# Hybrid layer with a hierarchical mixture of experts: one SiLU table in the expert loop, routing maxima in one pass, and the last projected rows in halves

## The reference, cut to what matters

```
h   = x + mix @ w_out                       # 1024 x 1024
t   = rms_norm(h, g)                        # h * rsqrt(mean(h*h) + eps) * g
g_logits = t @ w_rg + b_rg                  # 4 groups;    grp = argmax, p_grp = softmax(g_logits)[grp]
e_logits = t @ w_re + b_re                  # 16 experts, viewed as 4 groups of 4
e_in     = e_logits[grp]                    # the 4 experts of the chosen group
top_p, top_i = top_k(softmax(e_in), 2);  top_p = top_p / sum(top_p)
y  = sum over e of combine[:, e] * ( silu(t @ w_gate[e]) * (t @ w_up[e]) ) @ w_down[e]
out = h + y
```

## Time and profile before

| | us |
|---|---|
| median of 3 runs | 902.34 (901.07 to 904.18) |
| the profiled execution | 902.31 |
| its span | 900.5 |
| busy: TensorE, VectorE, ScalarE, GpSimd | 846.6, 623.4, 572.2, 234.7 |
| mean granted TensorE clock | 0.987 |

### The profile page before, as it was taken

One profiled execution on the slowest core, in us unless ns is written; L12 is line 12 of the kernel. 1 busy time (PEld: TensorE's weight loads), 2 busy tenths in 40 slices (PEclk: granted clock), 3 DMA queues, 4 the chain that ended last, 5 costly groups with the idle time before them and its releaser, 6 DMA issues.

```text
span 900.5 us, 19323 instructions
## 1 busy us (share of the span) xinstructions
PE 846.6 (94%) x5860; PEld 675.8 (75%) x5861; DVE 623.4 (69%) x1290; ACT 572.2 (64%) x1030; POOL 234.7 (26%) x421
## 2 busy tenths in 40 slices
PE   6999999999999999999988889999999999999993
PEld 4888888888888877788876667776668787777782
DVE  3866666666766687444579747783849799977991
ACT  3765564647374767122141768885869899888980
POOL 4101101010102010100041242545343444444450
PEclk9999999999999999999999999999989999999998
DMA  9801010101000162435392797867599999989962
GB/s 327 273 26 47 1 48 0 47 0 47 23 23 23 48 187 94 164 140 187 118 348 84 275 300 244 309 243 234 185 324 325 316 385 392 366 296 361 391 246 47
DMA packets 54736, 168.71 MB, mean 187 GB/s; under 512 B 9584, under 2 KB 11952, under 8 KB 54704
## 3 DMA queue, kind: packets, MB, share of 16 engines
q1 hardware_dynamic: 47312, 143.12, 43.3%
q0 software_dynamic: 7376, 25.18, 10.7%
q10 hardware_dynamic: 16, 0.01, 0.0%
HBM read 144.54 MB, written 23.75 MB: 187 GB/s over the span
## 4 chain that ended last, share of the span: by engine, by line
PE 57%; issue 16%; ACT 6%; DVE 6%; POOL 5%; DMA 4%; POOLq 2%; ACTq 1%; DVEq 1%; SPq 0%
PE bank_j L1093 11%; PE bank_j L1094 10%; PE bank_j L1095 10%; PE bank_j L1159 6%; ACT w_high L713 4%; PE bank_j L1165 3%; POOL tick L607 2%; DMA PT<-in_w_in_dram 2%; PE bank_o L1237 2%; PE bank_t L1231 2%; PE bank_t L1087 2%; POOLq L655 1%; PE bank_s L1546 1%; POOL hn L644 1%; DMA hn<-ffn_in,row_g 1%
## 5 line engine op out<-in xcount | busy, mean ns | idle before, releaser
L1093 PE MATMUL bank_j<-w_high,rows_high 128*128 128x512 f32 x512 | 206.9, 404 | 0.8 <-DVE rows_low L2189 0.6
L1094 PE MATMUL bank_j<-w_low,rows_high 128*128 128x512 f32 x512 | 200.8, 392 | 0.0
L1095 PE MATMUL bank_j<-w_high,rows_low 128*128 128x512 f32 x512 | 200.6, 392 | 0.0
L607 POOL TENSOR_TENSOR tick<-mhalf 1x1 f32<-1x1 f32 x192 | 78.1, 415 | 191.8 <-DVE lg L2202 76.2
L2090 DVE TENSOR_TENSOR w_low<-w_res,w_high 128x1024 fp32r<-128x1024 f32 x96 | 114.3, 1218 | 7.1 <-ACT w_high L713 7.1
L1093 PEld LDWEIGHTS bank_j<-w_high,rows_high 128*128 128x128 f32 x512 | 96.7, 189 | 28.9 <-issue 7.8
L1095 PEld LDWEIGHTS bank_j<-w_high,rows_low 128*128 128x128 f32 x512 | 96.7, 189 | 20.8
L1094 PEld LDWEIGHTS bank_j<-w_low,rows_high 128*128 128x128 f32 x512 | 96.9, 189 | 18.1 <-issue 0.2
L713 ACT ACTIVATE w_high<-w_res 128x1024 fp32r<-128x1024 f32 x96 | 97.6, 1051 | 0.0
L1159 PE MATMUL bank_j<-hnT,w_res 128*128 128x128 f32 x512 | 60.3, 277 | 0.0
L1159 PEld LDWEIGHTS bank_j<-hnT,w_res 128*128 128x128 f32 x512 | 58.4, 192 | 0.9
(11 more groups left out here) (392 smaller groups left out, 1824.9 us busy)
## 6 DMA issues: line engine op xcount, KB each, us to landing
w_res<-in_w_gate_dram SPq DMA_DIRECT2D x48, 512.0 KB, 6.7
w_res<-in_w_up_dram SPq DMA_DIRECT2D x48, 512.0 KB, 7.1
bias<-in_w_down_dram SPq DMA_DIRECT2D x32, 512.0 KB, 7.8
slot_b<-in_w_gate_dram SPq DMA_DIRECT2D x16, 512.0 KB, 10.2
PT<-in_w_up_dram SPq DMA_DIRECT2D x16, 512.0 KB, 10.8
gmix<-in_w_down_dram SPq DMA_DIRECT2D x16, 512.0 KB, 6.7
h<-in_w_down_dram SPq DMA_DIRECT2D x16, 512.0 KB, 8.2
hn<-in_x_dram SPq DMA_DIRECT2D x8, 512.0 KB, 3.3
```

What stands on the lines that cost most here:

```text
L607: pool.tensor_tensor(tick[:, len(ticks):len(ticks) + 1], mhalf[0:1, 0:1], mhalf[0:1, 0:1], ALU.mult)
L1093: pe.matmul(out_, ah, bh, start=start, stop=False)
L1094: pe.matmul(out_, ah, bl, start=False, stop=False)
L1095: return pe.matmul(out_, al, bh, start=False, stop=stop)
```

## The change

Three parts. (1) One dummy SiLU is placed ahead of the expert loop, behind the last exponential; those in `tile` and `small_tile` are taken out. (2) The router's 20 logits a row are seen as five groups of four (the group logits and each group's experts): one `first_max` finds all five maxima, a second finds each group's second expert, and the chosen group's mask is applied afterwards. (3) The last tile of projected rows is squared in two halves, whose sums GpSimd adds, scaled in two halves, and transposed and multiplied by the router weights in halves; two of the dummy matmuls ahead of it are dropped.

```diff
 (GpSimd, body2)
+                if last:
+                    pool.wait_ge(act_ssx, TILES + 1)
+                    pool.tensor_tensor(ssh[:, 1:2], ssh[:, 1:2], eps_d[:, 0:1], ALU.add).then_inc(pool_rx, 1)
+                    pool.wait_ge(pool_rx, TILES + 1)
                 pool.wait_ge(act_ssh, t + 1)
-                rsqrt(rsh[:, :], ssh[:, :], pool_rh, eps_d)
+                rsqrt(rsh[:, :], ssh[:, 0:1], pool_rh, ssh[:, 1:2] if last else eps_d)
 (ScalarE)
             def h2T_half(t):
-                act.wait_ge(pe_h2T, t + 1)
+                act.wait_ge(*((pe_hnT, TILES + 1) if isinstance(t, int) and t == TILES - 1 else (pe_h2T, t + 1)))
...
+                if last:
+                    act.wait_ge(dve_h0, t + 1)
+                    act.activation(junk[:, 0:HALF], xin[:, u, 0:HALF], ACT.Square, scale=float(D) ** -0.5,
+                                   accum_out=ssh[:, 1:2]).then_inc(act_ssx, 1)
                 act.wait_ge(dve_h, t + 1)
-                act.activation(junk, xin[:, u, :], ACT.Square, scale=float(D) ** -0.5, accum_out=ssh[:, :]).then_inc(act_ssh, 1)
+                cols = slice(HALF if last else 0, D)
+                act.activation(junk[:, cols], xin[:, u, cols], ACT.Square, scale=float(D) ** -0.5,
+                               accum_out=ssh[:, 0:1]).then_inc(act_ssh, 1)
...
             route_exp(TILES - EARLY, 2)
+            act.activation(warm[:, 0:1], warm[:, 1:2], ACT.Silu)
...
                 for i in range(2 * FC, PIECES):
                     split_hi(e, i, t - 1)
-                act.activation(warm[:, 0:1], warm[:, 1:2], ACT.Silu)
                 silu(t, 0)
...
             def small_tile(t, h):
-                act.activation(warm[:, 0:1], warm[:, 1:2], ACT.Silu)
 (TensorE)
-            def h2_T(t):
-                pe.wait_ge(dve_hn2, t + 1)
+            def h2_T(t, final=False):
+                pe.wait_ge(*((dve_hn, TILES + 1) if final else (dve_hn2, t + 1)))
...
                 for b, bank in enumerate((S0, S1)):
+                    if final and b == 1:
+                        ins.then_inc(pe_hnT, 1)
+                        pe.wait_ge(dve_hn2, t + 1)
...
                 pe.wait_ge(act_h2T, t + 1)
-                pe.wait_ge(dve_h2T, t + 1)
                 wait(pe, dve_rl, t)
                 for k in range(KC):
+                    if k == 4:
+                        pe.wait_ge(dve_h2T, t + 1)
...
-            keep_busy(18)
-            h2_T(TILES - 1)
+            keep_busy(16)
+            h2_T(TILES - 1, True)
 (VectorE, Route)
-                    gl = rl[:, a:b, 0:NG]
-                    self.ohg, gmx = self.first_max(gl, NG)
-                    tt(route_e[:, 0:T_ * NG].rearrange("p (t n) -> p t n", n=NG), gl, self.bc(gmx, NG), ALU.subtract)
-                    el = rl[:, a:b, NG:].rearrange("p t (g e) -> p t g e", g=NG)
-                    prod = new(T_ * NE).rearrange("p (t g e) -> p t g e", g=NG, e=EPG)
-                    tt(prod, el, self.ohg.unsqueeze(3).to_broadcast([P, T_, NG, EPG]), ALU.mult)
-                    ein = new(T_ * EPG).rearrange("p (t e) -> p t e", e=EPG)
-                    chain(dve.tensor_reduce(ein, prod.rearrange("p t g e -> p t e g"), AX, ALU.add))
-                    self.oh1, self.m1 = self.first_max(ein, EPG)
-                    self.e2 = new(T_ * EPG).rearrange("p (t e) -> p t e", e=EPG)
-                    chain(dve.scalar_tensor_tensor(self.e2, self.oh1, -3.0e38, ein, ALU.mult, ALU.add))
+                    every = rl[:, a:b, :].rearrange("p t (n w) -> p (t n) w", w=EPG)
+                    oh, mx = self.first_max(every, EPG, T_ * (1 + NG))
...
+                    tt(route_e[:, 0:T_ * NG].rearrange("p (t n) -> p t n", n=NG), rl[:, a:b, 0:NG],
+                       mx[:, :, 0:1].to_broadcast([P, T_, NG]), ALU.subtract)
+                    self.e2 = new(T_ * NE).rearrange("p (t g e) -> p t g e", g=NG, e=EPG)
+                    chain(dve.scalar_tensor_tensor(self.e2, self.oh1, -3.0e38,
+                                                   rl[:, a:b, NG:].rearrange("p t (g e) -> p t g e", g=NG),
+                                                   ALU.mult, ALU.add))
...
-                    oh2, m2 = self.first_max(self.e2, EPG)
-                    dve.tensor_tensor(route_e[:, T_ * NG:T_ * (NG + 1)], m2, self.m1, ALU.subtract).then_inc(dve_exps, 1)
+                    oh2, m2 = self.first_max(self.e2.rearrange("p t g e -> p (t g) e"), EPG, T_ * NG)
+                    diff = new(T_ * NG).rearrange("p (t g) -> p t g", g=NG)
+                    tt(diff, m2.rearrange("p (t g) -> p t g", g=NG), self.m1, ALU.subtract)
+                    tt(diff, diff, self.ohg, ALU.mult)
+                    dve.tensor_reduce(route_e[:, T_ * NG:T_ * (NG + 1)], diff, AX, ALU.add).then_inc(dve_exps, 1)
...
 (VectorE, body2: the last tile's scaling)
+                if last:
+                    dve.scalar_tensor_tensor(hv[:, :, 0:4], xv[:, :, 0:4], rsh[:, :], gv[:, :, 0:4], ALU.mult,
+                                             ALU.mult).then_inc(dve_hn, 1)
+                ks = slice(4 if last else 0, KC)
+                dve.scalar_tensor_tensor(hv[:, :, ks], xv[:, :, ks], rsh[:, :], gv[:, :, ks], ALU.mult,
                                          ALU.mult).then_inc(dve_hn2, 1)
```

More of the change, by code:

```diff
@@ L190, in hymba_layer_program @@
         hrs = sb("hrs", [P, MH])
-        ssh = sb("ssh", [P, 1])
+        ssh = sb("ssh", [P, 2])
         rsh = sb("rsh", [P, 1])
@@ L1621, in bc, with first_max @@
                     return v.unsqueeze(2).to_broadcast([P, self.T, w])
-                def first_max(self, vals, w):
-                    T_ = self.T
+                def first_max(self, vals, w, T_):
+                    bc = lambda v: v.unsqueeze(2).to_broadcast([P, T_, w])
                     mx, idx = new(T_), new(T_)
@@ L1628, in first_max @@
                     oh = new(T_ * w).rearrange("p (t n) -> p t n", n=w)
-                    tt(oh, vals, self.bc(mx, w), ALU.is_equal)
+                    tt(oh, vals, bc(mx), ALU.is_equal)
                     io, iom = (f[:, 0:w].unsqueeze(1).to_broadcast([P, T_, w]) for f in (iota_f[:, :], iota_m[:, :]))
@@ L1633, in first_max @@
                     chain(dve.tensor_reduce(idx, oh, AX, ALU.min))
-                    tt(oh, iom, self.bc(idx, w), ALU.is_equal)
+                    tt(oh, iom, bc(idx), ALU.is_equal)
                     return oh, mx
@@ new lines, in groups @@
+                    oh, mx = self.first_max(every, EPG, T_ * (1 + NG))
+                    oh = oh.rearrange("p (t n) w -> p t n w", n=1 + NG)
+                    mx = mx.rearrange("p (t n) -> p t n", n=1 + NG)
+                    self.ohg, self.oh1, self.m1 = oh[:, :, 0, :], oh[:, :, 1:, :], mx[:, :, 1:]
+                    tt(route_e[:, 0:T_ * NG].rearrange("p (t n) -> p t n", n=NG), rl[:, a:b, 0:NG],
+                       mx[:, :, 0:1].to_broadcast([P, T_, NG]), ALU.subtract)
+                    self.e2 = new(T_ * NE).rearrange("p (t g e) -> p t g e", g=NG, e=EPG)
@@ L1660, in masks @@
+                    diff = new(T_ * NG).rearrange("p (t g) -> p t g", g=NG)
+                    tt(diff, m2.rearrange("p (t g) -> p t g", g=NG), self.m1, ALU.subtract)
+                    tt(diff, diff, self.ohg, ALU.mult)
+                    dve.tensor_reduce(route_e[:, T_ * NG:T_ * (NG + 1)], diff, AX, ALU.add).then_inc(dve_exps, 1)
                     self.full = []
-                    for oh in (self.oh1, oh2):
+                    for oh in (self.oh1, oh2.rearrange("p (t g) e -> p t g e", g=NG)):
@@ L1662, in masks @@
                         self.full.append(new(T_ * NE))
-                        tt(self.full[-1].rearrange("p (t g e) -> p t g e", g=NG, e=EPG),
-                           self.ohg.unsqueeze(3).to_broadcast([P, T_, NG, EPG]),
-                           oh.unsqueeze(2).to_broadcast([P, T_, NG, EPG]), ALU.mult)
+                        ins = dve.tensor_tensor(self.full[-1].rearrange("p (t g e) -> p t g e", g=NG, e=EPG), oh,
+                                                self.ohg.unsqueeze(3).to_broadcast([P, T_, NG, EPG]), ALU.mult)
@@ L1666, in masks @@
+                    chain(ins)
                     dve.tensor_tensor(Mall[:, 0:T_ * NE], self.full[0], self.full[1], ALU.add).then_inc(dve_M, 1)
@@ L2077, in body2 @@
                 wait(dve, st_h2, 16 * t)
-                hv = h2[:, :].rearrange("q (k p) -> q p k", k=KC)
-                dve.scalar_tensor_tensor(hv, xin[:, u, :].rearrange("q (p k) -> q p k", k=KC), rsh[:, :],
-                                         gffn[:, :].rearrange("q (p k) -> q p k", k=KC), ALU.mult,
+                hv, xv, gv = (h2[:, :].rearrange("q (k p) -> q p k", k=KC), xin[:, u, :].rearrange("q (p k) -> q p k", k=KC),
+                              gffn[:, :].rearrange("q (p k) -> q p k", k=KC))
+                if last:
[3 more added lines that the diff above has]
+                dve.scalar_tensor_tensor(hv[:, :, ks], xv[:, :, ks], rsh[:, :], gv[:, :, ks], ALU.mult,
```

## The result

The changed kernel takes **897.51 us** in the median of 11 runs (894.99 to 899.6), beside 901.56 for the kernel before on the same chip. The ratio is 0.9949, 95% interval 0.9936 to 0.9963: 0.37% to 0.64% faster. The profiled execution took 896.47 us (span 894.4) where that of before took 902.31. Forecast were 898.2, within 895.0 to 902.0, and faster.

What follows compares the result with a forecast made beforehand. TensorE was taken as busy nearly throughout, with ScalarE close to the bound in the experts and a single path from 458 to 491 us. Terms of 1.30 + 0.92 + 0.8 + 0.36 + 0.69 = 4.1 gave 898.2 us, range 895.0 to 902.0.

Steps and rivals of the forecast that it cites:

- No load in the loop: Expert loop: with Silu set before it, every way in carries Silu, so all 42 ScalarE table loads there go.
- (b): Rival: ScalarE's time is hidden, loads stay in each body or VectorE starts late otherwise; 901.3 us, chance 0.15.
- Stalls behind small tiles: Full expert after two or three small tiles: without the first load TensorE's waits shrink by 1.30 and 0.92, together 2.2 us.
- Full behind full: Seven transitions from full expert to full expert: each gives 0.12, together 0.8 us, bounds 0 and 2.1.
- The closed loop: Between full experts: TensorE's transpose, ScalarE's copy, VectorE's subtraction, thirteen microseconds of VectorE to the hidden rows, next transpose.
- Head: Last projected rows and routing, before the first gather: 0.36 from halves plus 0.69 from routing, 1.05 us earlier.
- cover: Last projected rows: halved transposes and router matmuls gain nothing beside VectorE's weight subtractions; without those, up to 0.8 more.
- The early routing's 0: Five earlier tiles' routing, under the projection: 0.75 us longer second part just covered; taken as 0, loss at most 0.2.
- The first expert's 1.9: First expert: TensorE's 1.9 us wait for gated hidden rows, VectorE late for its own reasons; no gain, bounds 0 and 1.9.
- The sum: Whole kernel: 1.30 + 0.92 + 0.8 + 0.36 + 0.69 = 4.1 us, from 902.3 to 898.2.
- Rival (c): Experts: a shift of phase adds one more fall of TensorE's clock, costing 3.2 us; 901.4 us, chance 0.12.

Runs made afterwards that it cites:

- The load left at the head: Changed kernel with the dummy SiLU at the start of each tile and small tile, none ahead of the loop: 899.44 us, ratio 0.9977.
- the first pair: First profiled executions of the kernel before and the changed kernel, both unedited: 902.31 and 896.47 us.
- the second pair: Kernel before and changed kernel, each run again unedited: measured 901.41 and 897.01 us.
- routing only: Kernel before with only the new first_max, groups and masks: 901.47 us, ratio 0.9996.
- after again: Changed kernel run again, unedited: 897.01 us, ratio 0.9948.
- halves only: Kernel before with only the square, scaling, transposes and router matmuls in halves: 900.97 us, ratio 0.9992.

## Why the prediction was right, and where its steps were off

**No load in the loop**: shown, 42 loads to 1. The Trainium skill ("ScalarE activation tables: per-element evaluation and per-set limits", section "Table sets in the compiler and the runtime") has the loads placed per block, by the longest run. The prediction read this as a load that stays at the head of each body; the trace of the changed kernel has none there. The load left at the head prices that rival, (b): 2.1 us of gain, 1.1 of which the version without the tables' part has too, so about 1 of the tables' 3.2.

**Stalls behind small tiles** (1.30 + 0.92 forecast). The step to the 2nd full tile is 35.50 without stall or fall and 36.97 with the stall, 36.61 and 36.66 in two more traces that have it: 1.1 to 1.5. That to the 5th gained 0.81 in the first pair and 0.30 in the second. The load's part in the cause is shown by the load left at the head. The other part, a scatter that lands late, was not in the forecast, and the 0.92 of the fifth tile came from an execution in which it was late there; the 0.30 of the second pair is what that place gives without it. What the forecast missed besides is the third stall, in the 6th: 1.3 to 1.9 us in four traces whose clock is up there, worth 36.98 - 35.61 = 1.37 to 37.60 - 35.61 = 1.99 (37.60 is the step of routing only). The prediction counted waits in one trace, and there a clock fall covered it.

**Full behind full** (0.8 forecast): from the 6th to the 16th marker 204.30 went to 202.90, and 204.50 to 202.92: 1.4 to 1.6. The closed loop was the right one. The term was too small: it took the matmul at 767.25 and 0.04 at the transpose as all that TensorE lost in a step. A second matmul of before has the same excess, and both are gone after the change, which gives the 0.19 of a step, seven times 1.3. In the timeline of before, 0.34 from start to start where 0.23 is normal:
```profile
760.29 0.49 PE L1093 MATMUL bank_s<-w_high,hidden_high 128*128 128x512 f32 x1
760.63 0.40 PE L1094 MATMUL bank_s<-w_low,hidden_high 128*128 128x512 f32 x1
```
The first small tile behind a full one gains 0.1 to 0.3 as well (26.30 to 26.00, and 26.14 to 26.00, for the step to the 8th).

**Head** (0.36 + 0.69 = 1.05 forecast): 0.46 and 0.85 measured, 1.31. The mask chain is 0.76 of the latter, 3.77 us for 3.84 worked out. Of the halves' 0.46, the square gave 0.35 (addition to scaling 2.44 us, before 2.79) and the second scaling instruction took 0.06. Another 0.15 came where the prediction had seen cover: before, TensorE's transposes ended at 463.68, 0.02 behind VectorE's subtraction, and the copy of the transposed half stood at 1.28 behind the start of that subtraction; now it stands at 1.13. The indices have it whole. The early routing's 0 is shown, although the last addition starts at 457.69 and 458.34 in the traces of before and at 457.91 and 459.41 in those of after. From the last addition of the tile before (444.46, 445.11, 444.68, 446.20) to it there are 13.23, 13.23, 13.23 and 13.21 us. The scaling between them comes 0.30 later behind the one before it (13.57 for 13.27), and the addition doesn't move. In the first trace after, a fall of the clock at 485 to 491 then took 0.9 us of it from the transposes.

**The first expert's 1.9**, left out for reasons of VectorE's own: right, it stayed. It was also worth nothing, as the gather behind it shows.

**The sum** (4.1 forecast, 4.05 measured by the medians, 4.6 by the middle of the ratio). It is right partly by luck: with the stall that was missed and the full steps at their size the forecast would have been near 6 us, which the profiled executions show and the medians don't. By the places, the pieces of a loop without falls are 1.31 + 1.1 to 1.5 + 0.2 to 0.3 (2nd to 4th) + 0.3 to 0.8 + 1.4 to 2.0 + 1.4 to 1.6, about 6 us or more. The first pair of profiles differs by 5.84, the second by 6.16 (901.41 and 895.25). But the profiled execution of after lies 1.04 under its kernel's median and that of before 0.75 over its own, and 5.84 - 1.04 - 0.75 is the 4.05. Where a fall lies ahead of a stall of before, the change finds less to win; that this is what holds the medians under 6 was argued and not shown, since only profiled executions tell the place of a fall. The interval of the ratio is 3.3 to 5.8 us.

**Rival (c), falls that move**: half right. Falls come in the traces of both kernels (mean clock 0.987 in both first profiles, 0.993 in "after again"), so they are no price of the change but part of the spread under every run here.

## What to carry to other kernels

A load or any other fixed cost is worth what stands behind it in its queue, not its busy time: 42 loads, 54 us of ScalarE, were worth 3.2, while 30 loads at another place of the tile cost 28 to 31. Such a stall can need a second thing that is late only in some executions, here a scatter. Before counting an engine's waits, look at the granted clock of the stretch, since a slower TensorE hides the waits that a faster one has; profile the same kernel twice. And where a wait is removed ahead of a gather, ask first when the gather lands.

## What the runs showed of the hardware beyond that

TensorE's granted clock fell for some 3 to 7 us in the experts, at places that differ between executions of one kernel (659 to 668 and 527 to 533 us in two traces of before; 503 to 509 and nowhere in two of after). In halves only it followed a stretch of 3 us in which TensorE was busy 1.09; in "after again" the first expert's wait of 1.93 was followed by none. A step that held one was 1.6 to 3.1 us longer.
